# Attention of head and tile with both halves in one step, zero blocks written beside the dense product, and one modulation group moved into the attention stage

## What is computed

```python
sc = einsum('bhcqd,bhckd->bhcqk', q[..., q0:end, :], k[..., :end, :]) * scale   # c: the two halves
prob = softmax(where(causal, sc, neg), axis=-1)
attn = prob[:, :, 0] - lam * prob[:, :, 1]
block = einsum('bhqk,bhkv->bhqv', attn, v[:, :, :end])                         # 128 queries a block
o = rms_norm(o, subln_w) * (1.0 - lam_init)
```

## Time and profile before

| | us |
|---|---|
| median of 3 executions | 3782.99 |
| lowest and highest | 3777.36, 3788.05 |
| the profiled execution, its own time | 3777.18 |
| its span in the trace | 3775.4 |
| stage of the dense product, from its first split to its last matmul | 318.3 to 479 |
| stage of the heads, from SP's first transfer | 487.41 to 553.6 |
| stage of the attention, until the norm's first instruction | 553.6 to 626.6 |

### The profile page before, as it was taken

The page is one execution under the profiler, slowest core; times in us unless marked ns, Lnnn a source line. Parts: engine busy times, 40 slices in busy tenths (PEclk is TensorE's granted clock), DMA queues, the critical chain, the costliest instruction groups (busy, mean ns, idle before and its releaser), DMA issues. The chain is left out here.

```text
span 3775.4 us, 49915 instructions
## 1 busy us (share of the span) xinstructions
PE 3177.4 (84%) x18684; PEld 2591.6 (69%) x18684; DVE 2470.3 (65%) x2732; ACT 1925.2 (51%) x2169; POOL 561.3 (15%) x431
## 2 busy tenths in 40 slices
PE   7786957969999966778859999992998859999993
PEld 5685815758888855546648888881776658888883
DVE  3535236469999963454359999985225549999984
ACT  3322224147777743226227777762215527777762
POOL 0220000012222210000002222211004202222210
PEclk9898968979999988888959999996998969999997
DMA  4003267169999952450149999985211249999992
GB/s 124 1 4 90 73 225 263 51 242 366 372 373 373 365 207 91 161 203 2 57 160 361 377 374 381 375 302 208 77 45 27 60 150 370 369 365 365 362 349 105
DMA packets 227090, 832.64 MB, mean 221 GB/s; under 512 B 69734, under 2 KB 94182, under 8 KB 146300
## 3 DMA queue, kind: packets, MB, share of 16 engines
q1 hardware_dynamic: 195116, 786.16, 56.7%
q0 software_dynamic: 31680, 43.92, 3.4%
q10 hardware_dynamic: 144, 0.52, 0.0%
HBM read 816.53 MB, written 85.43 MB: 239 GB/s over the span
## 5 line engine op out<-in xcount | busy, mean ns | idle before, releaser
L184 DVE TENSOR_TENSOR f3e_w_lo<-f_raw,f3e_w_hi 128x2048 fp32r<-128x2048 f32 x198 | 446.4, 2285 | 4.8 <-ACT f3e_w_hi L179 4.8
L184 DVE TENSOR_TENSOR f2e_w_lo<-f_raw,f2e_w_hi 128x2048 fp32r<-128x2048 f32 x192 | 433.4, 2285 | 5.2 <-ACT f2e_w_hi L179 5.1
L184 DVE TENSOR_TENSOR f1e_w_lo<-f_raw,f1e_w_hi 128x2048 fp32r<-128x2048 f32 x192 | 432.9, 2285 | 5.9 <-ACT f1e_w_hi L179 5.9
L179 ACT ACTIVATE f3e_w_hi<-f_raw 128x2048 fp32r<-128x2048 f32 x198 | 371.0, 1910 | 0.2 <-issue 0.2
L179 ACT ACTIVATE f1e_w_hi<-f_raw 128x2048 fp32r<-128x2048 f32 x192 | 360.0, 1910 | 0.0
L179 ACT ACTIVATE f2e_w_hi<-f_raw 128x2048 fp32r<-128x2048 f32 x192 | 359.7, 1908 | 0.0
L190 PE MATMUL l_psum_acc<-l_w_hi,m_hT_hi 128*128 128x512 f32 x288 | 116.0, 403 | 33.3 <-DVE l_w_lo L184 33.3
L184 DVE TENSOR_TENSOR l_w_lo<-l_raw,l_w_hi 128x512 fp32r<-128x512 f32 x70 | 48.3, 692 | 122.2 <-ACT l_w_hi L179 122.2
L2006 POOL DMA_INDIRECT ybuf<-f3e_y,f_dst x32 | 67.5, 2109 | 340.7 <-DVE f3e_y L2212 330.2
L2006 POOL DMA_INDIRECT ybuf<-f1e_y,f_dst x32 | 67.6, 2112 | 339.6 <-DVE f1e_y L2212 329.1
L2006 POOL DMA_INDIRECT ybuf<-f2e_y,f_dst x32 | 67.5, 2109 | 338.7 <-DVE f2e_y L2212 328.2
(11 more groups left out here) (792 smaller groups left out, 8953.6 us busy)
## 6 DMA issues: line engine op xcount, KB each, us to landing
f_raw<-in_moe_w_dram SPq DMA_DIRECT2D x390, 1024.0 KB, 7.6
f_raw<-in_w_gate_dram SPq DMA_DIRECT2D x64, 1024.0 KB, 7.9
f_raw<-in_w_up_dram SPq DMA_DIRECT2D x64, 1024.0 KB, 7.4
f_raw<-in_w_down_dram SPq DMA_DIRECT2D x64, 1024.0 KB, 6.8
ybuf<-m_zeros SPq DMA_DIRECT2D x11, 2048.0 KB, 19.2
h_adaw<-in_ada_w_dram SPq DMA_DIRECT2D x16, 1024.0 KB, 6.9
he_adaw<-in_ada_w_dram SPq DMA_DIRECT2D x16, 1024.0 KB, 7.0
l_raw<-in_w_in_dram SPq DMA_DIRECT2D x56, 256.0 KB, 2.7
```

The lines of the kernel that those rows point to most:

```text
L179: return act.activation(dst, src, ACT.Copy)
L184: return v.tensor_tensor(dst, src, hi.bitcast(F32), ALU.subtract)
```

## The change

- The dense product is given the clearing: after the transfer of piece 6, 9, 12 and so on SP issues the next of the 13 writes, one at a time. `Clear.write` now issues one write a call (and before the first the two small reads), and `Clear.end` stands at the end of SP's stream in that stage.
- The attention stage is a new function, `difference_phase`. It has 16 jobs in place of 32, one for each head and tile, with both halves in it. The two halves' scores go into the two banks of one PSUM buffer. Mask, maximum and its negation are one instruction each for both halves. ScalarE does two exponentials, one for each half. VectorE then takes both reciprocals, forms the share -lambda * sum0 / sum1 (line 769 after) and adds share times the second half to the first (line 771 after). Only this difference is transposed, copied and multiplied by the values. ScalarE, not VectorE, scales it by the reciprocal of the first sum and writes the output. The pipeline is one job longer: TensorE's order is scores of job j, values of job j-3, transposes of job j-2.
- The modulation group (0, 1) is taken out of the heads' stage, which keeps (0, 0), and woven into the attention stage: eight pieces over 16 jobs.

The core of the diff (in the new function lines without a sign stood in `attention_phase` too, and the deleted lines of that function are in the listing above):

```diff
-def linear_phase(nc, name, parts, loads=(), RING=6, RAW=6, ahead=None):
+def linear_phase(nc, name, parts, loads=(), RING=6, RAW=6, ahead=None, clear=None):
...
                 if n == 0:
                     for dst, src in loads:
                         sp.dma_start(dst, src).then_inc(pre_in, 16)
+                if clear and n >= RAW and (n - RAW) % 3 == 0:
+                    clear.write(sp)
+            if clear:
+                clear.end(sp)
 
         @block.tensor
         def _(pe):
...
+def difference_phase(nc, name, tab, qT, kT, value, nlam, o, side=None):
+    jobs = [(h, t) for h in range(4) for t in range(NT)]
     nj = len(jobs)
     with Scope(nc, name) as s:
         psS = [s.ps(f"score{i}", 2) for i in range(2)]
+        psT = s.ps("turned")
         psO = [s.ps(f"out{i}") for i in range(2)]
+        pr = [s.sb(f"prob{i}", [P, 2, SEQ]) for i in range(2)]
+        prT = [s.sb(f"probT{i}", [P, SEQ]) for i in range(2)]
+        nm = s.sb("negmax", [P, nj, 2])
+        mx = s.sb("max", [P, nj, 2])
+        sm = s.sb("sum", [P, nj, 2])
+        rs = s.sb("rsum", [P, nj, 2])
+        share = s.sb("share", [P, nj])
+        s_done, max_done, exp_done, mix_done, t_done, ev, pv_done, post_done, own = (
+            s.sem(k) for k in ("s", "max", "exp", "mix", "t", "ev", "pv", "post", "own"))
+        extra = side(s) if side else None
         block = s.block()
+        def both(j, lo, hi):
+            return psS[j % 2][:, :].rearrange("p (c n) -> p c n", c=2)[:, :, lo:hi]
+        if extra:
+            @block.sync
+            def _(sp):
+                extra.begin(sp)
+                extra.sync(sp)
         @block.tensor
         def _(pe):
             def scores(j):
+                h, t = jobs[j]
                 if j >= 2:
+                    pe.wait_ge(exp_done, 2 * (j - 1))
+                n = (t + 1) * P
+                for c in range(2):
+                    mm = pe.matmul(both(j, 0, n)[:, c, :], qT[64 * c:64 * c + 64, h, t * P:(t + 1) * P],
+                                   kT[64 * c:64 * c + 64, h, 0:n], start=True, stop=True)
                 mm.then_inc(s_done, 1)
             def turn(j):
+                pe.wait_ge(mix_done, j + 1)
                 if j >= 1:
+                    pe.wait_ge(ev, j)
+                for k in range(jobs[j][1] + 1):
+                    mm = pe.transpose(psT[:, k * P:(k + 1) * P], pr[j % 2][:, 0, k * P:(k + 1) * P],
                                       tab[:, C_IDENT:C_IDENT + P])
                 mm.then_inc(t_done, 1)
             def values(j):
+                h, t = jobs[j]
+                pe.wait_ge(ev, j + 1)
                 if j >= 2:
                     pe.wait_ge(post_done, j - 1)
+                for k in range(t + 1):
+                    mm = pe.matmul(psO[j % 2][:, 0:P], prT[j % 2][:, k * P:(k + 1) * P], value(k, h),
+                                   start=(k == 0), stop=(k == t))
                 mm.then_inc(pv_done, 1)
+            for j in range(nj + 3):
                 if j < nj:
                     scores(j)
+                if j >= 3:
+                    values(j - 3)
+                if 2 <= j <= nj + 1:
+                    turn(j - 2)
+                if extra and j < nj:
+                    extra.tensor(pe, j, nj)
         @block.scalar
         def _(act):
+            if extra:
+                extra.prepare(act)
+            for j in range(nj + 3):
+                if j >= 3:
+                    i = j - 3
+                    h, t = jobs[i]
+                    act.wait_ge(pv_done, i + 1)
+                    act.activation(o[:, t, h * P:(h + 1) * P], psO[i % 2][:, 0:P], ACT.Copy,
+                                   scale=rs[:, i, 0:1]).then_inc(post_done, 1)
+                if 2 <= j <= nj + 1:
+                    i = j - 2
+                    n = (jobs[i][1] + 1) * P
                     act.wait_ge(t_done, i + 1)
                     if i >= 2:
                         act.wait_ge(pv_done, i - 1)
+                    act.activation(prT[i % 2][:, 0:n], psT[:, 0:n], ACT.Copy).then_inc(ev, 1)
                 if j < nj:
+                    n = (jobs[j][1] + 1) * P
                     act.wait_ge(max_done, j + 1)
+                    if j >= 2:
+                        act.wait_ge(t_done, j - 1)
+                    for c in range(2):
+                        act.activation(pr[j % 2][:, c, 0:n], both(j, 0, n)[:, c, :], ACT.Exp,
+                                       bias=nm[:, j, c:c + 1], accum_out=sm[:, j, c:c + 1]).then_inc(exp_done, 1)
+            if extra:
+                extra.scalar(act)
         @block.vector
         def _(v):
             link = Chain(v, own)
+            mask = tab[:, C_CAUS:C_CAUS + P].unsqueeze(1).to_broadcast([P, 2, P])
+            for j in range(nj + 1):
                 if j < nj:
+                    t = jobs[j][1]
+                    n = (t + 1) * P
                     v.wait_ge(s_done, j + 1)
+                    last = both(j, t * P, n)
+                    link(v.tensor_tensor(last, last, mask, ALU.add))
+                    link(v.tensor_reduce(mx[:, j, :], both(j, 0, n), AX.X, ALU.max))
+                    v.tensor_scalar(nm[:, j, :], mx[:, j, :], -1.0, None, ALU.mult).then_inc(max_done, 1)
+                if j >= 1:
                     i = j - 1
+                    n = (jobs[i][1] + 1) * P
+                    v.wait_ge(exp_done, 2 * j)
+                    link(v.reciprocal(rs[:, i, :], sm[:, i, :]))
+                    link(v.scalar_tensor_tensor(out=share[:, i:i + 1], in0=rs[:, i, 1:2], scalar=nlam[:, 0:1],
+                                                in1=sm[:, i, 0:1], op0=ALU.mult, op1=ALU.mult))
+                    v.scalar_tensor_tensor(out=pr[i % 2][:, 0, 0:n], in0=pr[i % 2][:, 1, 0:n], scalar=share[:, i:i + 1],
+                                           in1=pr[i % 2][:, 0, 0:n], op0=ALU.mult, op1=ALU.add).then_inc(mix_done, 1)
...
+        self.n, self.blocks = 0, SLOTS // 512
+        i = self.n
+        self.n += 1
+        if i == 0:
+            sp.wait_ge(self.zeroed, 2)
+            for k in range(2):
+                sp.dma_start(self.rp[:, k, 48:79], self.rel[k * 120:(k + 1) * 120, :]).then_inc(self.rel_in, 16)
+        if i < self.blocks:
+            dst = self.ybuf[512 * i:512 * i + 512, :].rearrange("(p j) d -> p (j d)", j=4).rearrange("p (j d) -> p j d", d=FF)
+        elif i < self.blocks + 2:
+            k = i - self.blocks
+            if k == 0:
+                sp.wait_ge(self.rel_in, 32)
+            sp.dma_start(self.relpad[k * 120:(k + 1) * 120, :].rearrange("r (c n) -> r c n", n=P),
+                         self.rp[:, k, :].unsqueeze(1).to_broadcast([120, 16, P])).then_inc(self.out, 16)
+        while self.n < self.blocks + 2:
+            self.write(sp)
+        sp.wait_ge(self.out, 16 * (self.blocks + 2))
...
                 linear(lhs, KD, allt, win[:, 1792:3328], 1536, copy_evac(lambda t, c: qkv[:, t, c * 512:(c + 1) * 512])),
-                linear(lhs, KD, allt, win[:, 3328:5376], 2048, gate_evac, on="a")])
+                linear(lhs, KD, allt, win[:, 3328:5376], 2048, gate_evac, on="a")], clear=clear)
...
-                side=lambda s: modulation.side(s, [(0, 0), (0, 1)], 3, first=True))
+                side=lambda s: modulation.side(s, [(0, 0)], 3, first=True))
...
-            attention_phase(nc, "a1", tab, jobs, clear)
+            difference_phase(nc, "a1", tab, qT, kT, lambda k, h: qkv[:, k, 1024 + h * P:1024 + (h + 1) * P], nlam, o,
+                             side=lambda s: modulation.side(s, [(0, 1)], 3))
```

94 lines of the change are left out of this document (removed).

## The result

The changed kernel takes 3736.5 us (median of four runs, 3732.2 to 3746.2), the kernel before 3781.6 (four runs beside it). The ratio is 0.9883, with a 95% interval from 0.9858 to 0.9908: 45 us less. The prediction was 3750, in a range from 3738 to 3768. The largest part of the miss is the first head of the attention stage, for which I had counted 18 us and which took 13.3. In a second series, on another chip, the same kernel took 3738.9 beside 3778.3 for the kernel before (0.989, 0.9873 to 0.9906), 39 us less.

The account below looks back on a forecast made before the run. TensorE was taken to bound the dense product, transfers the heads' stage, computing and clearing together the attention stage. Gains of 21.3 and 13.2 less 1 make 33.5 us: 3750 against the median of 3783.0, range 3738 to 3768.

Parts of the forecast that it names:

- Two ends of the attention stage: Attention stage: computing and the clearing's writes end together, so shortening one alone would give nothing.
- Heads' stage: Heads' stage: with eight of 16 pieces gone it ends at 532.3 instead of 553.6, a gain of 21.3 us.
- First head: Attention stage: first head at the lower clock takes 18 us, between 13 and 20.
- only the middle two can overlap: 3/4 of the time: Attention scores on TensorE: order c0 c0 c1 c1 overlaps only partly, so scores take 3.2 us a head instead of 4.3.
- higher clock from the start and full overlap: Attention stage, fast bound: 51 + 5 us, a gain of 17 us; no chance of its own.
- VectorE binds: Attention stage at the higher clock: VectorE is the longest at 10.3 us, taken as 10.6 a head with handoff.
- Rival 2: Attention stage: handoffs bind as before at 15.2 us a head; 19.7 us gained, 3763; chance 0.10.
- rival 1: Attention stage: TensorE's clock stays at its lower level throughout; 16.5 us gained, 3766; chance 0.10.
- Last head, drain and tail: Attention stage's end: last head 10.6 us, drain 5, then copies and stores 5.0.
- Dense product: Dense product: takes the clearing's writes with the queue at about 90%; 1 us lost, between 0 and 6.
- Rival 4: Dense product: weights wait behind the zeros, each of 13 writes costing TensorE 5.4 us; 36 us slower, 3819; chance 0.03.
- Rival 3: Heads' stage: stays bound by transfers, each piece 2 us late; 17.5 us gained, 3765; chance 0.04, with rival 2 0.03.

Follow-up runs that it names:

- The clearing alone: Changed kernel with the old 32-job attention and both modulation groups in the heads' stage, clearing in the dense product: 3780.3 us, ratio 1.000.
- the new attention alone: Changed kernel with the clearing back in the attention stage and both modulation groups in the heads' stage: 3780.9 us, ratio 0.9993.
- both together: Changed kernel with both modulation groups in the heads' stage, none in the attention stage; clearing in the dense product: 3754.3 us, ratio 0.9934.
- The kernel with the same rows: Changed kernel with both halves' scores computed from rows 0 to 63, so that they can't overlap: 3749.3 us, ratio 0.9904.
- the 32 jobs with the modulation: Changed kernel with the old 32-job attention and modulation group (0, 1) woven into it: 3767.7 us, ratio 0.9966.
- the two kernels with more writes: Changed kernel with a clearing write after every weight transfer, 3766.6 us (0.9964), or every second, 3744.4 us (0.9906), instead of every third.

## What held of the prediction, and the step that failed

**Two ends of the attention stage: right.** The clearing alone gave 0.0%, the new attention alone 0.07%, both together 0.66%, and in the changed kernel the stage ended with computing and its tail.

**Heads' stage: right, 1.2 us short.** From SP's first transfer I had VectorE's eighth tile at 523.3 - 487.4 = 35.9 us; it was ready at 526.67 - 490.52 = 36.2. I had the copies begin at 38.6 (526), they began at 37.4 (527.91). Then 2.4 and 3.9 us followed as worked out. So the term that was too large is the 2.7 us of TensorE between: I had put a piece at the lower clock (1.89) and the bias there. The clock was at its higher level by then (a piece takes 1.04), and the bias stood beside VectorE's last instructions (525.55 to 526.58, tile ready at 526.67).

**First head: the step that failed.** I took 2 x 8.2 = 16.4 and 1.6 for the start, 18 us; it was 13.3. This term is 4.7 of the missing 8.1 us. By the runs it falls into three parts, of which the sizes are estimates.

- The overlap, 2.1 us. The prediction reasoned that of c0 c0 c1 c1 "only the middle two can overlap: 3/4 of the time". Four instructions of 512 columns took 1.13, against 1.98 for the same four from the same rows: the halves overlap in full. With half the time for the scores my own count gives 7.15 a head instead of 8.2, and 15.9 for the first one.
- The work that doesn't stand in the first head, 2.4 us. I had put a whole head's count there. By TensorE's order the first head has four jobs' scores and two pieces, but only the first job's values and the transposes of the first two; the rest falls behind it. The kernel with the same rows shows it by itself: without any overlap and at the lower clock throughout, my count gives 2 x 9.3 + 1.6 = 20.2, and its first head took 17.7. With the overlap and the lower clock for 12.1 of its 13.5 us, the changed kernel in its second profile lies as far below 15.9. Against this stood longer waits at the start: 1.4 us for the bias and 2.5 for the first piece, where I had 1.6 in all. That the piece lands 6 us after the stage's start was right (540.18 - 534.25).
- The clock, 0.3 us: 13.5 with its rise after 12.1 us, 13.3 with its rise after 9.2.

**The clock itself was wrong too, and cost the forecast little.** I counted on a rise 22 to 24 us in, "the same now", as I compared by TensorE's busy share. It rose 8.1 to 12.2 us in, in all nine profiles of kernels with the two halves side by side, and 23.7 to 25.7 us in, in the four with one half after another (before, the clearing alone, the 32 jobs with the modulation, the same rows), in which TensorE was the busier. The same-rows experiment changes nothing but the rows that are used, so these make the difference. As my 18 us for the first head were at the lower clock and all that follows at the higher, the early rise could give only what it saved in the first head. I had "higher clock from the start and full overlap" as the end of the attention's bounds, with a stage of 56 us, but gave it no rival and no chance of its own; at 54.1 the stage went beyond even that bound, though the clock was not high from the start.

The Trainium skill, "TensorE: Matmul & The Clock Gate", in its section on packing small matmuls, says that matmuls in distinct row groups run concurrently. I had weighed it with 3/4 against half; the trace after agrees with the page, 1.13 against 1.98 us. What the page's rule was worth beyond my 3/4 I had put at 2 us, and that was right for the first head; set against no overlap at all it is worth 12.4 us of the stage, about 4 of them through the clock.

**VectorE binds: only in part, 1.3 us short over two heads.** The durations of VectorE's instructions add up to 9.4 us a head, against 9.3 worked out. The 10.3 to 10.6 stood on 0.04 us for each chained step and some handoff on top. But an instruction that doesn't need its forerunner's result starts before that one's end (the reciprocal at 575.00, the negation at 574.92 for 0.17), so VectorE is busy only 8.8 us a head, and without modulation a head took 8.8 and 9.2 us. With it a head takes 9.95, and TensorE is busy 97% of that, 9.6 us. I had 8.2 for TensorE and compared it with 10.3 to 10.6 for VectorE, and so named the wrong engine as the last. The 8.2 was too low, although the overlap is better than I took it to be: in the same-rows kernel, where my count is 9.3, TensorE was busy 11.4 of the 11.5 us of the third head. One part of it shows in the trace before: the values start 1.05 us after the scores of 512 keys (588.85 to 589.90), where I had 0.85. Rival 2, handoffs of 15.2 a head, fell, and so did rival 1: the clock stayed up for three heads.

**Last head, drain and tail: right.** From the fourth head's start to the copies it took 16.0 us (567.40 to 583.44) for a predicted 15.6, and from there to the next stage 4.9 for 5.0.

**Dense product: right in its number, wrong in its reasons.** I took 1 us and found 0.1. But "no split is late" was wrong: several were, by up to 4.6 us (6.75 of waiting in place of 2.17). And the slack was "16.8 us and the six pieces in hand", 33 us; the two kernels with more writes showed 13 and 11. The step that was wrong here is the landing: I had a transfer behind a write land after 8 us, and it took up to 14.7, so most of the 16.8 us was gone by the landing alone. A write and three pieces took 7.95 us and not 7.4, so the queue was at 95% of TensorE's pace and not at 90. Rival 4 was to decide from 2.7 us a write on. By an estimate from these runs it decides once a write with its three pieces takes more than 8.40 plus 12 / 13, that is 9.3 us, 1.4 above what it takes. The change stood nearer to that edge than I said.

**Rival 3, a heads' stage still bound by transfers: fell.** Eight pieces were issued in 23.5 us, and VectorE's pace of 2.73 held to the last tile.

**The sum.** Heads' stage 1.2, first head 4.7, second and third 1.3, last head with drain and tail -0.4, dense product 0.9, and 0.4 in the small stage for lambda, which I had left out: 8.1, as between 33.5 and 41.6. (The heads' stage of before is itself uncertain by 1 to 2 us, see above.) The remaining 3.5 of the 45 us are in stages that the change doesn't touch. In the second series they had the other sign: 39.4 for 41.0 in its four stages.

## What to carry to other kernels

Where two things end a stage at the same time, removing either gives nothing, and such a change is to be costed and tested whole: here 0, 0 and, both together, 26 us. Matmuls that use half of the array's rows are worth pairing on distinct rows: here 12.4 us of a stage of 66.5, two thirds of it by the overlap and a third because the clock rose earlier. Where a pipeline fills, count for its first stretch only the work that stands in it. Writes can be put beside a stage that TensorE bounds as long as write and loads together stay under TensorE's pace for the same loads; beyond that each lost microsecond shows once the pieces in hand are used up. How much is in hand depends on how late a load lands behind a write, so read this from a trace with the writes in it.
